# Mixture block with a gated delta solve on one core: the two modulation chunks of a solve level are split around the right product, and some work of the last tile is moved

## What is computed

```python
m_lat = split(silu(c) @ w_mod + b_mod, 6)       # likewise m_ctx, and w_mod_2 for block two
# gated delta rule, chunked; per tile of tokens, head and direction:
lower = where(strict, kb @ k.T * decay, 0)
t_inv = triangular_solve(eye + lower, eye)      # u = t_inv @ (v * beta), w = t_inv @ (kb * exp(gc))
v_new = u - w @ s;  o = q_dec @ s + qk @ v_new;  s = s * g_last + k_dec.T @ v_new
y = rmsnorm(o_forward + o_backward, norm_g) * silu(gate)
o_df = rmsnorm(diff_attention(...), df_g) * (1 - lam_init)
x = x + m_lat[2] * (concat(o_na, y, o_df, o_ft) @ w_out)
```

## Time and profile before

| | us |
|---|---|
| median of 3 runs (lowest to highest) | 2306.96 (2306.05 to 2314.09) |
| the profiled execution, device time | 2308.12 |
| its span, first to last instruction | 2306.3 |
| PE busy in it | 1898.4 (82%) |
| DVE busy in it | 509.6 (22%) |

### The profile page before, as it was taken

One profiled execution on the slowest core, in us unless ns is written; L12 is line 12 of the kernel. 1 busy time (PEld: TensorE's weight loads), 2 busy tenths in 40 slices (PEclk: granted clock), 3 DMA queues, 4 the chain that ended last, 5 costly groups with the idle time before them and its releaser, 6 DMA issues.

```text
span 2306.3 us, 30312 instructions
## 1 busy us (share of the span) xinstructions
PE 1898.4 (82%) x12166; PEld 1059.0 (46%) x12166; DVE 509.6 (22%) x1047; ACT 319.9 (14%) x592; POOL 97.7 (4%) x125
## 2 busy tenths in 40 slices
PE   6999998867676767676766767799999599999997
PEld 3676776742222222222222222688788344444443
DVE  3224563330000000000000000342521312222222
ACT  3123331010000000000000000211520100000001
POOL 1012211000000000000000000000200000000000
PEclk9999999867667677777677676799999799999999
DMA  8214556079999999999999999244344699999997
GB/s 337 90 38 165 206 200 229 34 288 423 422 422 422 422 422 422 422 422 422 423 422 422 422 422 422 100 135 144 122 144 148 262 418 421 422 422 422 422 422 295
DMA packets 102752, 728.67 MB, mean 316 GB/s; under 512 B 11440, under 2 KB 12048, under 8 KB 16144
## 3 DMA queue, kind: packets, MB, share of 16 engines
q1 hardware_dynamic: 99504, 717.04, 76.4%
q10 hardware_dynamic: 3168, 10.49, 1.3%
HBM read 726.39 MB, written 1.10 MB: 315 GB/s over the span
## 4 chain that ended last, share of the span: by engine, by line
PE 66%; DMA 24%; DVE 4%; issue 3%; ACT 2%; POOL 0%; DVEq 0%; SPq 0%; ACTq 0%; POOLq 0%
DMA ring<-in_w_down 18%; PE psum L499 9%; PE psum L712 9%; PE psum L851 7%; PE psum L487 5%; PE psum L746 4%; DMA ring<-in_w_mod 4%; PE psum L1147 3%; PE psum L526 3%; PE psum L723 2%; PE psum L693 2%; DMA ring<-in_moe_w 2%; PE psum L1136 2%; PE psum L1081 2%; PE psum L979 2%
## 5 line engine op out<-in xcount | busy, mean ns | idle before, releaser
L499 PE MATMUL psum<-ring,main 128*32 128x512 f32 x2048 | 277.7, 692 | 85.0 <-ACT main L573 35.0
L518 PE MATMUL psum<-ring,main 128*32 128x512 f32 x1024 | 176.1, 808 | 84.8 <-DMA ring<-in_w_down 72.4
L712 PE MATMUL psum<-ring,main 128*64 128x512 f32 x1024 | 226.4, 594 | 2.3 <-DMA ring<-in_moe_w 1.3
L499 PEld LDWEIGHTS psum<-ring,main 128*32 128x32 f32 x2048 | 65.2, 123 | 281.0 <-issue 184.5
L851 PE MATMUL psum<-main,ring 128*128 128x256 f32 x768 | 169.2, 380 | 0.0
L851 PEld LDWEIGHTS psum<-main,ring 128*128 128x128 f32 x768 | 146.0, 190 | 21.7 <-issue 0.5
L712 PEld LDWEIGHTS psum<-ring,main 128*64 128x64 f32 x1024 | 72.5, 137 | 151.1 <-issue 149.8
L487 PE MATMUL psum<-main 128*128 128x32 f32 x512 | 112.5, 402 | 33.8 <-DVE main L551 33.8
L487 PEld LDWEIGHTS psum<-main 128*128 128x128 f32 x512 | 110.4, 332 | 57.5 <-DVE main L551 57.5
L518 PEld LDWEIGHTS psum<-ring,main 128*32 128x32 f32 x1024 | 30.7, 134 | 211.0 <-DMA ring<-in_w_down 145.1
L558 DVE TENSOR_TENSOR main<-main,psum 128x512 f32<-128x512 f32 x16 | 11.0, 688 | 525.1 <-ACT main L576 525.1
(11 more groups left out here) (422 smaller groups left out, 2056.5 us busy)
## 6 DMA issues: line engine op xcount, KB each, us to landing
ring<-in_moe_w SPq DMA_DIRECT2D x192, 1024.0 KB, 17.0
ring<-in_w_gate SPq DMA_DIRECT2D x128, 1024.0 KB, 25.9
ring<-in_w_up SPq DMA_DIRECT2D x128, 1024.0 KB, 25.9
ring<-in_w_down SPq DMA_DIRECT2D x128, 1024.0 KB, 20.4
ring<-in_w_mod SPq DMA_DIRECT2D x48, 1024.0 KB, 6.9
ring<-in_w_in SPq DMA_DIRECT2D x36, 1024.0 KB, 4.9
ring<-in_w_out SPq DMA_DIRECT2D x8, 1024.0 KB, 5.7
ring<-in_w_rnn_out SPq DMA_DIRECT2D x8, 640.0 KB, 3.9
```

Of the source, the lines that this page charges most:

```text
L499: last = mm(psum[32 * j:32 * j + 32, b, :], xg1[:, k, :], slot(n % SLOTS)[:, 512 * j:512 * j + 512], start=k == 0, stop=k == KT - 1)
L518: last = mm(psum[q:q + 32, BANK_Y, :], hidT[:, P * (f % 4) + 32 * (f // 4):P * (f % 4) + 32 * (f // 4) + 32], w[:, r, 512 * g:512 * g + 51 ...
L712: last = nc.tensor.matmul(psum[CAP2 * u:CAP2 * u + CAP2, b, :], xg2[:, 4 * h + k, CAP2 * u:CAP2 * u + CAP2], w[u][:, k, :], start=h == 0 a ...
```

## The change

The modulation pair of a level is split: `mod_pair` takes `halves`. Chunk 0 of pair `n` is now multiplied in `fill_early(n)`, after the scores, and chunk 1 in `fill_mods(n)`, for all of `n` = 0 to 19. The bank is allocated with chunk 0, and is full with chunk 1. In the last tile, `df_sums` and `df_norm` move ahead of DVE's wait for the right product of levels 1 and 2, and `mix_turn(2)` moves in level 3 between the left and the right product. The end list is written in another order. The gain of the norm is multiplied into the gate after level 6 of tile 2, and the two gating products at the end become one, on `o_acc`, ahead of the wait for the reciprocal root.

```diff
-                 "end": [("ws", 2, 1, 3), ("ws", 3, 0, 3), ("wo", 0, 3), ("so", 2, 1, 3), ("so", 3, 0, 3),
-                         ("wo", 1, 0), ("ws", 3, 1, 2), ("wo", 1, 1), ("so", 3, 1, 2),
+                 "end": [("wo", 0, 3), ("ws", 2, 1, 3), ("ws", 3, 0, 3), ("wo", 1, 0), ("so", 2, 1, 3), ("so", 3, 0, 3),
+                         ("wo", 1, 1), ("ws", 3, 1, 2), ("so", 3, 1, 2),
                          ("wo", 1, 2), ("wo", 1, 3)]}
-            def mod_pair(b, p):
+            def mod_pair(b, p, halves=(0, 1)):
                 key = ("mod", b, p)
-                t = banks.new(key)
-                pe.wait_ge(*banks.free(key))
-                for i in range(2):
+                if 0 in halves:
+                    banks.new(key)
+                    pe.wait_ge(*banks.free(key))
+                t = banks.tile(key)
+                for i in halves:
...
-                last.then_inc(banks.when_full(key), 1)
+                if 1 in halves:
+                    last.then_inc(banks.when_full(key), 1)
             def fill_early(n):
                 if n < NA_N:
                     scores(n)
-                elif n < len(PAIRS):
-                    mod_pair(*PAIRS[n])
+                if n < len(PAIRS):
+                    mod_pair(*PAIRS[n], (0,))
             def fill_mods(n):
-                if n < NA_N:
-                    mod_pair(*PAIRS[n])
+                if n < len(PAIRS):
+                    mod_pair(*PAIRS[n], (1,))
# PE, in level (3, 3): mix_turn(2) moves from behind the level's fillers to here
                     fill_early(n)
+                    if (t, lv) == (3, 3):
+                        pe.wait_ge(df_ready, 1)
+                        mix_turn(2)
# DVE: df_sums, df_norm move from behind the recurrence steps to here
                     attend(n)
+                    if (t, lv) == (3, 1):
+                        df_sums()
+                    if (t, lv) == (3, 2):
+                        df_norm()
                     dve.wait_ge(*banks.full(("p", t, lv)))
...
+                    if (t, lv) == (2, 6):
+                        g8 = gate_tm.rearrange("p t (h n) -> p (t h) n", h=H)
+                        V.tensor_tensor(g8, g8, M("dn_norm").unsqueeze(1).to_broadcast([P, NT * H, HD]), ALU.mult).then_inc(dve_step, 1)
# DVE, at the end
-            for t in range(NT):
-                g4 = gate_tm[:, t, :].rearrange("p (h n) -> p h n", h=H)
-                V.tensor_tensor(g4, g4, M("dn_norm").unsqueeze(1).to_broadcast([P, H, HD]), ALU.mult).then_inc(dve_step, 1)
-                dve.wait_ge(dve_step, dve_steps())
+            V.tensor_tensor(o_acc.rearrange("p t h n -> p (t h n)"), o_acc.rearrange("p t h n -> p (t h n)"),
+                            gate_tm.rearrange("p t n -> p (t n)"), ALU.mult).then_inc(dve_step, 1)
+            dve.wait_ge(dve_step, dve_steps())
             dve.wait_ge(head_rstd, 1)
             for t in range(NT):
...
-                dve.wait_ge(dve_step, dve_steps())
-                V.tensor_tensor(mix[:, t, 256:512], mix[:, t, 256:512], gate_tm[:, t, :], ALU.mult).then_inc(dve_step, 1)
```

More of the change, by code:

```diff
@@ L1478, in _ @@
                         mix_turn(0)
-                    if (t, lv) == (3, 3):
-                        pe.wait_ge(df_ready, 1)
-                        mix_turn(2)
                 pe.wait_ge(full_ready, t + 1)
@@ L2370, in _ @@
                             new_values(step, d, u)
[L2371 to L2374, removed]
                     if (t, lv) == (3, 5):
```

## The result

| | before | changed |
|---|---|---|
| median us (lowest to highest, runs) | 2310.25 (2306.05 to 2314.09, 4) | 2339.51 (2335.24 to 2357.09, 4) |
| span of the profiled execution, us | 2306.3 | 2335.6 |
| PE busy in the solve stretch, us | 190.4 | 210.5 |
| PE waiting for chunks in it, us | 14.0 | 34.6 |

The changed kernel is slower by the ratio 1.0146 (95% interval 1.0118 to 1.0174), estimated from all the runs; the two medians alone stand at 1.0127, which is 29.3 us. The two spans differ by 29.3 us too. One run of the last experiment, at 2498 us with a mean granted clock of 0.73 where all others had 0.84 or more, is left out everywhere. The prediction of 2322.6 us had the direction; its range ended at 2333 and did not hold the time.

A forecast was written before the change was run, and what follows sets the result against it. It took PE's own work plus PE's waits to bound the solve stretch (184 to 389.9 us). Terms: 19.5 + 6 - 4.8 - 5.1 = 15.6 us more, from the median 2306.96 to 2322.6 us; range 2311 to 2333.

The forecast's parts named there:

- The waits: Solve levels: PE waits 31.5 us for chunks in place of 14.0, plus 2 for slow loads: 19.5 us more.
- The clock: Solve, behind the new waits: four falls of PE's clock at about 1.5 us each, 6 us more; bounds nothing and 13.
- the second rival: Clock falls in most waits of 1.8 and 2.3 us, end gives no clock: 25 us more, 2332; chance 0.23.
- Bank and hidden waits: Left products of levels 7, 10, 13, 16: PE about 0.3 us too soon for the bank ACT copied; costs 0.
- Level (3, 3): Last tile: right product's wait shrinks by 2.5 us, low clock behind it goes, 2.3 us; together 4.8 us less.
- The end: End list and gating: 1.8 us net of waits, 2.4 of clock, 0.9 of DVE's gating products; 5.1 us less.
- The first rival: Waits come, clock stays up in all levels, end has full gain: 5 to 11 us more, 2312 to 2318; chance 0.23.
- The third: Solve levels: first chunk lands before PE wants it, so the 14.0 us of waits go too: 2283; chance 0.04.

The follow-up runs named there:

- the last experiment: The new end list and the gating moves alone, on the kernel before; 2302.0 us, ratio 0.9984.
- the first experiment: The changed kernel with the modulation pairs whole and back in their old places, other moves kept; 2299.43 us, ratio 0.9938 to the kernel before.
- the run with the filler: The changed kernel plus unneeded identity transposes into the pair's bank ahead of the wait for chunk 0; 2320.44 us, ratio 1.0040 to the kernel before.
- the run with its own release: The changed kernel, with chunk 0's slot free for reload once chunk 0 is multiplied, not when the bank is full; 2286.86 us, ratio 0.9886.

## Why the prediction was off, point by point

**The waits: right.** Forecast were 31.5 us, with 2 more for slow loads; measured are 34.6, in 19 waits, all at first chunks but one. Level 2 has 1.61 us for a forecast of 1.8, level 8 2.57 for 2.3, level 17 4.05 for 3.8. Three places were off. Level 1 waits 2.65 us for a forecast of 1.8, as no pair stands before it whose transposes come first. Level 12 waits 1.27 where none was forecast: its load took 6.9 us to landing, one of the slow ones for which the 2 us stood. And the second chunk of level 18, whose load took 8.5 us, is waited for by 0.96, where no second chunk was to be. One row was misread without harm: the 7.0 us of the earlier trace rows belong to the load issued at 348.9, and the successor of that issued at 205.62 took 8.3.

**The clock: mis-sized, and this is the step that failed.** The prediction took "four falls, 6 us", at "about 1.5 us" each. There were eight, and they cost 18.5 us, 17.2 more than the one fall of the kernel before. Two things were wrong in it. The first is the count. The prediction weighed 2.3 us against single rows, one wait of 2.15 that left the clock up and one of 2.87 that did not. In the changed kernel a wait of 1.97 us (level 10) was followed by a fall, and one of 2.41 (level 11) was not:

```profile
313.56 1.75 PE L1083 MATMUL psum<-ring,main 128*32 128x256 f32 x16 [1.97 <-DMA ring<-in_w_mod]
...
325.73 1.07 PE L1083 MATMUL psum<-ring,main 128*32 128x256 f32 x16 [2.41 <-DMA ring<-in_w_mod]
```

The length of a single wait does not sort these cases. With the split alone two waits of 1.68 us (levels 3 and 4) stand side by side, the first followed by a fall and the second not, and with the split in the late levels a wait of 2.80 us (level 16) left the clock up. The second, and as large, is the length of a fall. The price of 1.5 us is that of 3.4 us at the low clock, which is what the kernel before had in level 16, and the five falls of that length cost 1.3 to 1.6 us here. But three falls lasted 6.8 to 10.2 us, with PE busy in them from the end of the wait on, and cost 11 us together. The row that said so was among those read, 13.5 us at 0.50 with PE busy for 12.7 of them. It was used for the second rival, and not for the price. Eight falls by the 2.3 us that the forecast itself had found behind the wait of 3.07 us would have been 18 us. Its upper bound of 13 us (nine by 1.5) was also built on the short fall, so it was no bound.

With the measured terms the sum is 20.6 + 17.2 + 3.5 - 4.9 - 6.9 = 29.5 us, where the forecast had 19.5 + 6 - 4.8 - 5.1 = 15.6. The 3.5 us are the small terms behind the table above, which the forecast did not have. The clock alone is 11 of the 14 us missed. The changed kernel went the way of the second rival, many falls, and further than its 25 us, though that rival had denied the end its gain of clock, and it came.

**Bank and hidden waits: right.** Two waits of 0.2 us for ACT's copy, at the left products of levels 7 and 13, where about 0.3 was forecast in four levels; chunk 0 is waited for behind both.

**Level (3, 3): right.** Forecast 4.8 us less, measured 4.9, with a wait of 0.55 us where under 1 was forecast.

**The end: right, a little small.** Forecast 5.1 us less, measured 6.9. The new wait is 0.69 us (0.75 forecast), and those of 0.70 and 1.86 us are gone: 1.9 us net for 1.8. The first two `ws` behind the dense `wo` ran at the high clock, as hoped, in 3.9 us for 6.85 before: 3.0 for 2.4. The two gating products gave 0.8 us for 0.9. What the sum lacked is that the `uw` products and the three `wo` up to the last `so` had also run partly at the low clock before; they take 1.2 us less. The rest of the end is as forecast: "nothing behind `mix_ready` changes". The wait before the last product is shorter, 2.22 us in place of 3.13, but no time is won by that. The product hangs on ACT's copy, and starts 3.91 us behind the end of DVE's last product ahead of `mix_ready` (483.06 to 486.97), where it was 3.90 (453.66 to 457.56). The wait shrank because the double `wo` ahead of it ran partly at a low clock and took 7.09 us. In the first experiment it took 5.40, the wait was 3.12, and the stretch from the first `uw` was the same 32.9 us:

```profile
438.04 5.40 PE L1436 MATMUL psum<-ring,main 128*128 128x256 f32 x24
...
447.79 9.63 PE L1436 MATMUL psum<-ring,main 128*128 128x256 f32 x32 [3.12 <-ACT main L1611]
```

**The first rival**, that the clock stays up, is what the run with the filler brought about: it measured 2320.4 us, where the rival had 2312 to 2318. **The third**, that the first chunk lands in time, is what the run with its own release made true: 2286.9 us, where the rival had 2283. Both came near in size, the first in part by luck, since it counted on the whole gain at the end and had no work added; the changed kernel just was neither.

## What to carry to other kernels

A buffer that is split in use must be split in its release too: ask for each load what signal lets it start, and whether an edit moves its first use nearer to that signal. Where a change adds many waits of about two microseconds to an engine whose clock is granted, price the clock by all the low stretches of the profile, the long ones with a busy engine too, and not by the shortest, and let the range hold several long ones. An engine's busy time for the same number of instructions, 210.5 against 190.4 us here, shows at once about how much of a loss is clock (17.2 of those 20.1 us) and how much is waiting.

## What the runs showed of the hardware

The clock stayed down while PE was dense: in level 8 PE was busy for 9.7 of 10.2 us at a granted clock of 0.51, and in level 13 (351.6 to 358.4 us) for all of 6.8. Behind like waits it came back after 3.4 us elsewhere (level 9, a wait of 2.59 us). What decides between the two is open; no run here was made for it. The clock did not follow the length of a single wait either: it fell with waits of 1.68 and 1.97 us and stayed up with others of 1.68, 2.41 and 2.80.

Eight small transposes, 1.04 us of PE's time, in each of eleven levels, with 12 and 20 in two more, kept the clock at 1.00 through the whole solve, with 16.7 us of waits still in it, the longest 1.9 us. Work without a use made the kernel 19 us faster than without it.

Of two loads of 1 MB that the changed kernel issued 0.4 us apart, the first landed 4.6 to 6.9 us behind its issue and the second 6.7 to 8.9, with a median of 6.8 over both; with its own release, where no two were issued together, the median was 5.0.
